# A down projection by seven block products: sums of weights and of features prepared beside TensorE

## The reference

```python
h2 = rms_norm(x, g_ffn_pre[i])
u = causal_dwconv(h2 @ w_up[i], conv_w[i], conv_b[i])      # 1024 -> 2 x 2816
ug, uv = u[..., :D_FF], u[..., D_FF:]                      # D_FF = 2816 = 22 x 128
f = (jax.nn.gelu(ug, approximate=True) * uv) @ w_down[i]   # 512 x 2816 by 2816 x 1024
x = x + rms_norm(f, g_ffn_post[i])
pg = jax.nn.sigmoid(rms_norm(x, g_ple_pre[i]) @ w_ple_gate[i])
x = x + rms_norm(pg * (p[i] @ w_ple[i]), g_ple_post[i])
```

## Time and profile before

| | us |
|---|---|
| median of 3 runs | 1843.96 (1843.73 to 1844.3) |
| span of the profiled execution | 1842.0 |
| TensorE busy (rows of matmuls) | 1833.6, 100% |
| VectorE busy | 1038.2, 56% |
| ScalarE busy | 884.6, 48% |
| GpSimd busy | 164.1, 9% |
| transfers | 183.66 MB, mean 100 GB/s |
| down projection, first layer | 744.7 to 864.4 |
| down projection, second layer | 1656.7 to 1776.4 |

### The profile page before, as it was taken

One profiled execution on the slowest core, in us unless ns is written; L12 is line 12 of the kernel. 1 busy time (PEld: TensorE's weight loads), 2 busy tenths in 40 slices (PEclk: granted clock), 3 DMA queues, 4 the chain that ended last, 5 costly groups with the idle time before them and its releaser, 6 DMA issues.

```text
span 1842.0 us, 26192 instructions
## 1 busy us (share of the span) xinstructions
PE 1833.6 (100%) x9243; PEld 1528.1 (83%) x9243; DVE 1038.2 (56%) x1658; ACT 884.6 (48%) x1552; POOL 164.1 (9%) x178
## 2 busy tenths in 40 slices
PE   9999999999999999999999999999999999999998
PEld 8888888788888888888898888887888888888887
DVE  4756555545577767324656565555445777763244
ACT  4676546533454444224547764465335444442253
POOL 1002000011011111001010020001111111110010
PEclk9999999999999999999999999999999999999999
DMA  6322353234323333323243224532342333333322
GB/s 184 77 81 84 106 106 95 61 95 161 103 81 102 91 101 93 125 92 97 85 148 88 64 83 112 104 93 64 95 168 81 103 91 102 91 102 115 103 81 80
DMA packets 280164, 183.66 MB, mean 100 GB/s; under 512 B 62564, under 2 KB 262912, under 8 KB 279808
## 3 DMA queue, kind: packets, MB, share of 16 engines
q1 hardware_dynamic: 279688, 182.13, 34.2%
q10 hardware_dynamic: 376, 0.21, 0.1%
HBM read 175.68 MB, written 4.46 MB: 98 GB/s over the span
## 4 chain that ended last, share of the span: by engine, by line
PE 99%; DVE 0%; ACT 0%; issue 0%; DVEq 0%; POOL 0%; POOLq 0%; ACTq 0%
PE psum L791 89%; PE psum L1022 2%; PE psum L1003 2%; PE psum L988 2%; PE psum L834 1%; PE psum L975 1%; PE psum L974 1%; PE psum L1000 0%; PE psum L985 0%; PE psum L1212 0%; PE psum L984 0%; PE psum L803 0%; PE psum L820 0%; PE psum L1272 0%; DVE xnl L1743 0%
## 5 line engine op out<-in xcount | busy, mean ns | idle before, releaser
L791 PE MATMUL psum<-xnh,wh 128*128 128x512 f32 (+1 forms) x1424 | 563.8, 396 | 0.0
L791 PE MATMUL psum<-xnh,wl 128*128 128x512 f32 (+1 forms) x1424 | 548.6, 385 | 0.0
L791 PE MATMUL psum<-xnl,wh 128*128 128x512 f32 (+1 forms) x1424 | 548.0, 385 | 0.0
L1729 DVE TENSOR_TENSOR wl<-raw,wh 128x1024 fp32r<-128x1024 f32 (+1 forms) x272 | 355.1, 1306 | 292.9 <-ACT wh L1330 292.8
L1330 ACT ACTIVATE wh<-raw 128x1024 fp32r<-128x1024 f32 (+1 forms) x272 | 284.0, 1044 | 363.7 <-PE psum L791 349.1
L791 PEld LDWEIGHTS psum<-xnh,wl 128*128 128x128 f32 x1424 | 267.5, 188 | 54.6
L791 PEld LDWEIGHTS psum<-xnh,wh 128*128 128x128 f32 x1424 | 269.0, 189 | 50.4 <-issue 2.7
L791 PEld LDWEIGHTS psum<-xnl,wh 128*128 128x128 f32 x1424 | 268.2, 188 | 46.7
L1854 DVE CUSTOM_DVE_ANT_0 Sp<-psum,ptok 128x128 f32<-128x128 f32 (+3 forms) x128 | 62.7, 491 | 108.7 <-issue 61.7
L791 PE MATMUL psum<-wh,fh 128*128 128x512 f32 x288 | 112.0, 389 | 0.0
L791 PE MATMUL psum<-wh,fl 128*128 128x512 f32 x288 | 112.0, 389 | 0.0
(11 more groups left out here) (281 smaller groups left out, 2901.2 us busy)
## 6 DMA issues: line engine op xcount, KB each, us to landing
raw<-in_w_up_dram SPq DMA_DIRECT2D x88, 512.0 KB, 3.7
raw<-in_w_gate_dram SPq DMA_DIRECT2D x48, 512.0 KB, 3.7
raw<-in_w_down_dram SPq DMA_DIRECT2D x44, 512.0 KB, 3.5
raw<-in_w_in_dram SPq DMA_DIRECT2D x30, 512.0 KB, 3.9
raw<-in_w_out_dram SPq DMA_DIRECT2D x16, 512.0 KB, 3.5
raw<-in_w_ple_gate_dram SPq DMA_DIRECT2D x16, 512.0 KB, 4.2
rx<-rspill SPq DMA_DIRECT2D x48, 128.0 KB, 2.9
raw<-in_w_in_dram SPq DMA_DIRECT2D x16, 260.0 KB, 3.0
```

What stands on the lines that cost most here:

```text
L791: ins = pe.matmul(out, left, right, start=start and n == 0, stop=stop and n == 2)
L1729: dve.tensor_tensor(low[:, 0:n], raw[(L * NCH + c) % RAW][:, 0:n], hi[:, 0:n].bitcast(F32), ALU.subtract).then_inc(w_lo.sem, 1)
```

## The change

**Seven products.** Tokens are halved (A: 0 to 255, B: 256 to 511), so are the output columns (left, right), and the 22 feature tiles form 11 pairs of an even and an odd tile (PAIRS). A product of 2 x 2 blocks takes eight block products; here it takes seven, of sums and differences of blocks (Strassen's scheme in one of its variants). A block product for one pair is 2 blocks of 128 tokens x 512 columns x 3 passes = 6 matmuls.

**Two rounds.** Round one goes over the 11 pairs with two chunks each and makes four products (12 matmuls per chunk): `dn_raw` holds two corners of the pair's weights as they are, `dn_rows` sums of rows. Round two goes over the pairs again and makes three: `dn_cols` holds sums of columns (12 matmuls), `dn_diff` the difference of the two corners (6 matmuls, 512 wide). So there are 44 chunks instead of 22. The corners are read twice. In round one their halves have four buffers (`dn_near`, in the place of xnh). The last three pairs of round two (6 chunks) have buffers of their own and are taken product by product.

**Sums of weights.** Row sums are made by VectorE in the raw buffers (`rows_sum`, before the low half of the corners; it needs both chunks landed), except the first pair's. These and all column sums are made in DRAM: GpSimd, after its memsets at the start of each layer, copies half of w_down (5.8 MB, and 0.5 MB of rows) to a DRAM buffer, waits for that, and adds the other half to it by transfers with accumulation. Differences are made by VectorE in the raw buffers (`diff`).

**Sums of features.** GpSimd makes them in the up projection (`features_apart`: one difference of 512 for round one, three pieces, 768 in all, for round two, and the low halves). ScalarE makes the high half of the difference (`cross_hi`) between its other work; for the last pair this is ahead of the high half of chunk 3. The 768 columns for round two go to DRAM (`qspill`) and come back as 384 KB per pair into two raw buffers (`q_raw`). ScalarE and VectorE split them (`sums_hi`, `sums_lo`) beside chunks 6, 8, ... 18, 26, 28, 30 and 32, since their place is taken by `fh` and `fl` until a pair of round one is done.

**End.** Products of round one are copied and added between the rounds (`products_out`, `threes_taken`, `fours_taken`); the residual follows the tail's products (`down_rest`, `down_roots`). `gain_down` is loaded at chunk 30, `gain_pg` at the layer's last load.

```diff
+PAIRS = FT // 2
+CHUNKS += [(k, j) for j in range(PAIRS) for k in ("dn_raw", "dn_rows")]
+CHUNKS += [(k, j) for j in range(PAIRS) for k in ("dn_cols", "dn_diff")]
...
+DN_TAIL = 3
+DN_SLOTS = 4
+DN_TAIL_AT = 4 * PAIRS - 2 * DN_TAIL
...
+Q_PREP = [2 * j + 6 for j in range(7)] + [26, 28, 30, 32]
...
@@ SP, behind load(L, c): @@
-                if c == ST_DOWN + 10:
-                    wait(w_used.sem, w_used.at(L, ST_DOWN + 4))
+                for j in range(PAIRS):
+                    if c == ST_UP + 4 * j + 11:
+                        wait(q_ready.sem, q_ready.at(L, j + 1))
+                        sp.dma_start(qspill[L, :, j, :], f_sums[:, :]).then_inc(q_spilled.sem, 16)
+                    if c == ST_DOWN + Q_PREP[j] + 3:
+                        if j == 0:
+                            wait(f_lo.sem, f_lo.at(L, 3 * PAIRS))
+                        wait(q_spilled.sem, q_spilled.at(L, 16 * PAIRS) if j == 0 else q_spilled.at(L, 16 * (j + 1)))
+                        if j >= 2:
+                            wait(q_lo.sem, q_lo.at(L, j - 1))
+                        sp.dma_start(q_raw[j % 2][:, :], qspill[L, :, j, :]).then_inc(q_back.sem, 16)
+                if c == ST_DOWN + 30:
+                    wait(w_used.sem, w_used.at(L, ST_DOWN + 2 * PAIRS))
                     gain_load(L, 1, "g_ffn_post")
...
@@ TensorE, round one, one pair (c = ST_DOWN + 2 * j): @@
+                for a in range(2):
+                    ins = product(two[a], c, 0, hi, lo, 768, a, first, last)
...
+                for a in range(2):
+                    ins = product(five[a], c, 1, hi, lo, 512, a, first, last)
...
+                for a in range(2):
+                    ins = product(three_[a], c + 1, 1, hi, lo, 0, a, first, last)
...
+                for a in range(2):
+                    ins = product(four[a], c + 1, 0, hi, lo, 256, a, first, last)
...
@@ ScalarE: @@
+        def sums_hi(L, j):
+            act.wait_ge(q_back.sem, q_back.at(L, 16 * (j + 1)))
+            act.wait_ge(w_used.sem, w_used.at(L, ST_DOWN + 2 * j + 2))
+            act.activation(qh[:, j, :], q_raw[j % 2][:, :], ACT.Copy).then_inc(q_hi.sem, 1)
...
+        def down_chunks(L):
+            for n in range(3, 4 * PAIRS + 2):
+                hi(L, ST_DOWN + n)
+                if n in Q_PREP:
+                    sums_hi(L, Q_PREP.index(n))
+                if n == 2 * PAIRS + 1:
+                    products_out(L)
+                if n == 31:
+                    half_sums(L)
...
             hi(L, ST_DOWN + 1)
+            hi(L, ST_DOWN + 2)
             up_post(L, -1, 2 * FT // 4)
-            for c in range(ST_DOWN + 2, ST_PG):
-                hi(L, c)
+            cross_hi(L, PAIRS - 1)
+            down_chunks(L)
...
@@ VectorE: @@
+        def rows_sum(L, c):
+            own, rows = (L * NCH + c) % RAW, (L * NCH + c + 1) % RAW
+            dve.wait_ge(w_landed[own], LAND[L * NCH + c])
+            dve.wait_ge(w_landed[rows], LAND[L * NCH + c + 1])
+            dve.tensor_tensor(raw[rows][:, :], raw[rows][:, :], raw[own][:, :], ALU.add
+                              ).then_inc(rows_made.sem, 1)
...
+        def down_chunks(L):
+            for n in range(3, 4 * PAIRS):
+                q = n - 2 * PAIRS
+                if q >= 0 and q % 2 == 0:
+                    diff(L, q // 2)
+                if n == 2 * PAIRS + 2:
+                    threes_taken(L, 0)
+                    threes_taken(L, 1)
+                lo(L, ST_DOWN + n)
+                if n == 2 * PAIRS + 3:
+                    fours_taken(L, 0)
+                    fours_taken(L, 1)
+                if n in Q_PREP:
+                    sums_lo(L, Q_PREP.index(n))
...
@@ GpSimd: @@
+        def weight_sums(L):
+            rows = A["w_down"].rearrange("l (j m p) c -> l m p j c", m=2, p=P)
+            cols = A["w_down"].rearrange("l (t p) (h c) -> l h p t c", p=P, h=2)
+            pool.dma_start(row_sums[L], rows[L, 0, :, 0:1]).then_inc(wsum_copied.sem, 16)
+            pool.dma_start(col_sums[L], cols[L, 0]).then_inc(wsum_copied.sem, 16)
+            pool.wait_ge(wsum_copied.sem, wsum_copied.at(L, 32))
+            pool.dma_start(row_sums[L], rows[L, 1, :, 0:1], max_dma_last_dim=4096, accum_op=ALU.add).then_inc(wsum_in.sem, 16)
+            pool.dma_start(col_sums[L], cols[L, 1], accum_op=ALU.add).then_inc(wsum_in.sem, 16)
```

More of the change, by code:

```diff
@@ L88 @@
 SPL = 2
-TAIL = {"out": 4, "down": 4, "pg": 6}
+TAIL = {"out": 4, "pg": 6}
 EXTRA = {}
-for _s, _n in ((ST_OUT, KT), (ST_DOWN, FT), (ST_PG, KT)):
+for _s, _n in ((ST_OUT, KT), (ST_PG, KT)):
     for _e in range(TAIL[CHUNKS[_s][0]]):
@@ L94 @@
 EXTRA.update({2: 0, 3: 1})
-RING = [c for c in range(NCH) if c not in EXTRA]
+DN_TAIL = 3
+DN_SLOTS = 4
+DN_TAIL_AT = 4 * PAIRS - 2 * DN_TAIL
+DN_NEAR = {ST_DOWN + n: n % DN_SLOTS - SPL for n in range(DN_TAIL_AT) if n % DN_SLOTS >= SPL}
+DN_LATE = {ST_DOWN + n: n - DN_TAIL_AT for n in range(DN_TAIL_AT, 4 * PAIRS)}
+RING = [c for c in range(NCH) if c not in EXTRA and c not in DN_NEAR and c not in DN_LATE]
 assert len(RING) % SPL == 0
@@ L107 @@
 FW = 340
-WIDTH = {"first": 2 * FW}
+WIDTH = {"first": 2 * FW, "dn_diff": 512}
 F_GATE, F_PE, F_VC = 512, 520, 552
-G_OF = {"first": 0, "out": 0, "down": 0, "pg": 0, "uqn": 2, "uqp": 2, "ukn": 0, "ukv": 4, "ple": TB,
+G_OF = {"first": 0, "out": 0, "dn_raw": 0, "dn_rows": 0, "dn_cols": 0, "dn_diff": 0, "pg": 0, "uqn": 2, "uqp": 2, "ukn": 0, "ukv": 4, "ple": TB,
         "branch0": 2, "branch1": 2, "branch2": 2}
@@ L618, in chunk_dmas @@
         raise ValueError(kind)
-    N_DMA = [{"first": 3, "qC": 2, "uqn": 4, "uqp": 8, "ukn": 2, "ukv": 2}.get(k, 1) for k, _ in CHUNKS]
+    N_DMA = [{"first": 3, "qC": 2, "uqn": 4, "uqp": 8, "ukn": 2, "ukv": 2, "dn_rows": 2}.get(k, 1) for k, _ in CHUNKS]
     LAND = []
@@ L636, in load @@
             wait(w_lo.sem, w_lo.at(L, c - RAW + 1))
+            if CHUNKS[c] == ("dn_rows", 0):
+                wait(wsum_in.sem, wsum_in.at(L, 32))
             n = 0
@@ L867, in turn_all @@
         def turn_all(L):
-            for t in range(1, TB):
-                block_free(L, 1, t)
+            pe.wait_ge(rest_made.sem, rest_made.at(L, TB))
             for t in range(TB):
@@ L1725, in lo @@
                 return
+            if CHUNKS[c][0] == "dn_raw" and CHUNKS[c][1] > 0:
+                rows_sum(L, c)
             dve.wait_ge(w_hi.sem, w_hi.at(L, c + 1) + it * 4)
@@ L2189, in _ @@
                 lo(L, c)
-            residual(L, 0)
+            residual(L)
             pre_norm_lo(L, 1, V_FFNPRE, 1)
@@ L2213, in _ @@
             links[0] = after + 2
-            for c in range(ST_DOWN + 2, ST_PG):
+            down_chunks(L)
+            for c in range(ST_PLE, ST_PG):
                 lo(L, c)
-            residual(L, 1)
+            down_rest(L)
             lo(L, ST_PG)
@@ new lines, in down_roots @@
+        def down_roots(L):
+            pool.wait_ge(half_summed.sem, half_summed.at(L, TB))
+            link(pool.tensor_scalar(ysums[:, 0, :], ysums[:, 0, :], EPS, None, ALU.add))
+            for i, t in enumerate(DN_ORDER):
+                one = slice(t, t + 1)
+                pool.wait_ge(rest_summed.sem, rest_summed.at(L, i + 1))
+                link(pool.tensor_tensor(ysums[:, 2, one], ysums[:, 0, one], ysums[:, 1, one], ALU.add))
+                inverse_root(rpost[:, one], ysums[:, 2, one]).then_inc(root_done.sem, 1)
@@ L2288, in _ @@
         pool.wait_ge(f_lo.sem, 1)
+        pool.sem_inc(q_spilled.sem, 16)
         for L in range(DEPTH):
```

408 lines of the change are left out of this document (331 added, 77 removed).

## The result

Before: 1843.88 us (median of 4). After: **1944.82 us** (median of 4; 1941.98 to 1947.31). The ratio is 1.0546, 95% interval 1.0531 to 1.0561: slower, as forecast, but by 101 us where 30 were forecast, and outside the range.

What follows compares the result with a forecast made beforehand. TensorE, with 99% of the chain, was taken as the bound. Per layer, -15.0 for matmuls and the waits gave +14.6, DRAM sums +0.5; twice that, +30, on 1842.0 plus 2.0 gave 1874 us, range 1857 to 1894.

Steps and rivals of the forecast that it cites:

- the loop: Down stage: reading and splitting feature sums takes 7.4 us, then 6.7, where TensorE needs 5.44 and 4.08; 1874, chance 0.62.
- DRAM sums: Layer start: GpSimd's copy and addition of weights in DRAM fit beside other transfers; 0.5 us a layer.
- Matmuls removed: Down projection: 462 matmuls a layer instead of 528, saving 15.0 us a layer if nothing waits.
- Rival 4: DRAM sums late: GpSimd's wait holds window queries, or first chunks' loads; 10 to 25 us more, near 1890; chance 0.12.
- Entry: Start of the down stage: TensorE waits 4.1 us for chunk 3; with chunks 4 and 7, +5.1 us a layer.
- Round one: Down stage, first four products: six waits of 2.0 us from the 7.4 us loop, +11.8 us a layer.
- round two: Down stage, last three products: 6.7 us loop against 4.08, TensorE loses 9.2 us a layer by chunk 34.
- tail: End of round two: three column chunks wanted within 1.4 us, the third late; wait of 3.5 us a layer.
- rival 5: Clock: waits of 4 us could drop TensorE to 1.2 GHz, 2.7 us more some ten times; near 1890; chance 0.06.
- Rival 2: Down stage: transfers or port are the bound, stage 144 to 148 us; 1892 to 1901; chance 0.10.
- Rival 3: Down stage: waits for the sums are covered, only the entry stays; faster, 1824 to 1830; chance 0.10.

Runs made afterwards that it cites:

- e1: Changed kernel without GpSimd's copies and additions in DRAM, unsummed rows of w_down read instead: 1913.39 us.
- e2: Kernel before the change, with only the bursts of DRAM sums added at each layer's start and their result unread: 1874.41 us.
- e5: Changed kernel without DRAM sums, reads of feature sums early, chunk 3's high half ahead, round one's sums conversions two chunks later: 1855.07 us.
- e3: Changed kernel with the reads of feature sums, but the first, issued two chunks earlier, a semaphore per buffer: 1885.27 us.
- e10: e5 with nine of a layer's eleven reads of feature sums left out, old buffers converted again: 1844.86 us.
- e16: e11 with the gain row's transfer and products later, last four PSUM reads behind chunks 27 and 31, squares back ahead of chunk 32: 1843.56 us.
- e11: Whole changed kernel with DRAM sums in paced pieces, early reads, chunk 3's high half ahead, later sums conversions, late squares: 1852.65 us.

## Why the prediction was wrong, point by point

The direction and the loop were right, the size was not. Two steps of the sum failed: the DRAM sums at 0.5 a layer, where they cost 15.7, and the loop's waits priced with every matmul at full clock, where the stage has 14 us more of busy time than its matmuls need.

- **Matmuls removed, -15.0 a layer.** Right: 463 matmul rows in the window, 0.227 us apart at full clock.
- **DRAM sums, "so it fits; I take 0.5 a layer".** This step failed: 16 and 19 us (e1: 31.4 for both; e2: 15.2 each). The durations were foreseen (a copy of 25 us, an addition of 25 to 50; measured 24 and 41). The error was to ask if they end before GpSimd is wanted again, with the mean transfer share of a long window. The question was how much the loads still get beside them, and for how long: 1.55 MB of 7.8 beside the copy, and 14.9 us for a load, not "5 for 3.5". That sentence leaned on the Trainium skill, DMA: Bandwidth & Descriptors, Queues, rings and completion order (engines take turns by packet). Turns by packet need not be equal shares of bytes: beside the copy a packet of GpSimd's queue held 4.3 KB and one of the loads' queue 0.5. Half the rate, an estimate from that page of 7 us at worst, is borne out by no run here, neither beside the copy nor beside the addition; the measurement decides. Rival 4 was this mechanism, priced at 10 to 25 in all (measured 31), with 0.12: too low for a price that no row bounded.
- **Entry, +5.1.** Right in place, a little low: waits of 1.15 us for chunk 1 (forecast none; ScalarE made its high half 1.4 us later than forecast, behind the last GELU), 3.33 for chunk 3 and 1.71 at the first sums (788.25): 6.2. The 0.4 that was added to three or four instructions of VectorE beside GpSimd (the forecast's "port cost") was right: four of them, from 772.46 to 778.76, took 1.7 us more than elsewhere. But the repair of the entry in e5 brought nothing measurable while later bounds stood.
- **Round one, +11.8; round two, +9.2; tail, +3.5.** The mechanism was right (e3 took it away, 59.5 us), sizes a little low. The loop was 8.1 and 7.2, not 7.4 and 6.7; the mis-sized term is the read of the sums, 5.2 us from the low half to the landing and not 4.3. Its first round took longer still, 10.0 us in the first layer (from 785.92 to 795.92). Tail waits were 2.39 and 3.40, so 5.8. All idle time is 33.0 against 29.6. By e3 the loop is worth 30 a layer against 21 forecast: idle time fell by 21.1 and 18.2 us, and busy time by 8.8 and 9.2.
- **The clock (rival 5, 0.06, "near 1890").** This step failed too: the sum has nothing for it. It was not an alternative to the loop but came with it: of the 14 us a layer of excess busy time some 10 are matmuls 0.43 us apart, and e3, which took the waits away, left 3.5 us of them in its first stage. Chances were split between cases that come together. By its own terms, 2.7 us some ten times, the rival's time was 1901 and not 1890. The Trainium skill, TensorE: Matmul & The Clock Gate, Part 1, has that idleness lowers the clock; the trace agrees, at 0.66 in the window with the 4.27 us wait. No run held the waits and lifted the clock, so this price rests on the rows alone.
- **Rival 2, transfers.** Not the bound of the change (share 0.58), but the next one behind the loop: e10.
- **Rival 3, covered.** False; even in e16, with the loop and the DRAM sums mended and the entry shortened, nothing is won.

Sum a layer: 17 above the step for DRAM, 14 of excess busy time, 3.5 of waits: 34.5, twice 69, and the miss was 71.

Open: what the last 7.6 to 9.5 us of waits in e16 would need. The first two pairs of the tail are ready 3.8 us apart there (TensorE's waits for them end at 845.20 and 848.96; 4.2 us in e11). More raw buffers were not tried.

## What to carry to other kernels

Saving TensorE's work raises the pace that everything else must keep: here four chunks lasted 21.8 us and now 10.9 or less, against a loop of 5.8, and each transfer, order and PSUM read that used to be covered came up in turn, until the 15 us a layer were spent. Price a big background transfer by the bytes that the loads still get beside it and by how long that lasts, and issue it in pieces of half a megabyte between other work: same bytes, 30 us against none. When TensorE is forecast to wait again and again, add the slow matmuls behind the waits to the same case.

## What the runs showed of the hardware

- An accumulating transfer from DRAM to DRAM, 6.3 MB in one go, ran 41 us (150 GB/s, beside 69 of loads) with the engines saturated; a plain copy of as much ran 24 us (262, beside 65). Loads of 512 KB beside them landed after 14.9 us (median), of 256 KB after 24.1.
- The same in pieces of 512 KB landed in 6.0 us and cost nothing, at a transfer share of up to 0.87 over 50 us.
- Waits of 2.4 to 2.9 us on TensorE stood in windows of 10 us with the granted clock at 1.00 in some and 0.83 in others; behind 3.3 us it was 0.90, behind 4.3 us 0.66, and 0.66 again where waits of 2.4 and 3.4 us stood in one window.
- VectorE and GpSimd held each other up from 772.5 to 778.8 us of the changed kernel: VectorE's low halves and sums of 1024 columns start 1.14 us apart elsewhere and up to 1.7 there, and GpSimd's low half of 512 columns took 2.27 us where it took 1.30 in the up projection.
